# An mLSTM head's output transposes moved from behind the third to behind the fourth output-gate unit

## The reference

```python
hm = mlstm_chunkwise(mq, mk, mv, i_pre, logf)
hm = hm * lax.rsqrt(jnp.mean(hm * hm, axis=-1, keepdims=True) + EPS)
hm = (hm.reshape(B, S, M_WIDTH) * m_norm_w[l]).astype(x.dtype)
hm = hm * jax.nn.sigmoid(mo)
y_m = (hm * jax.nn.silu(mz)) @ w_m_branch[l]
```

## Time and profile before

| what | value |
|---|---|
| time, median of 3 runs | 1391.82 us (1391.68 to 1391.87) |
| time of the profiled execution | 1391.64 us |
| its span, first to last instruction | 1389.9 us |
| mean granted TensorE clock | 0.992 |
| tensor engine busy | 1328.2 us, 96% |
| vector engine busy | 668.1 us, 48% |
| ScalarE busy | 397.0 us, 29% |
| GpSimd busy | 662.6 us, 48% |

### The profile page before, as it was taken

The page is one execution under the profiler, slowest core; times in us unless marked ns, Lnnn a source line. Parts: engine busy times, 40 slices in busy tenths (PEclk is TensorE's granted clock), DMA queues, the critical chain, the costliest instruction groups (busy, mean ns, idle before and its releaser), DMA issues.

```text
span 1389.9 us, 20009 instructions
## 1 busy us (share of the span) xinstructions
PE 1328.2 (96%) x6846; PEld 1128.8 (81%) x6846; DVE 668.1 (48%) x1297; ACT 397.0 (29%) x926; POOL 662.6 (48%) x854
## 2 busy tenths in 40 slices
PE   3499999999999999999999999999999999999997
PEld 2398797989877888889978987898789888688886
DVE  5979886785873000153265235424542321544335
ACT  5334445353450100023322332333132311311111
POOL 6834507061366544295267146715661455557340
PEclk9799999999999999999999999999999999999999
DMA  9411102010021220230131031103210132321502
GB/s 350 123 45 31 47 2 61 15 32 28 0 61 61 75 79 26 89 93 17 48 89 30 0 90 46 30 0 92 59 30 15 45 92 91 106 91 61 197 16 106
DMA packets 119832, 89.30 MB, mean 64 GB/s; under 512 B 13305, under 2 KB 111721, under 8 KB 118894
## 3 DMA queue, kind: packets, MB, share of 16 engines
q1 hardware_dynamic: 116288, 76.16, 17.9%
q10 hardware_dynamic: 3502, 12.61, 2.6%
HBM read 80.35 MB, written 8.41 MB: 64 GB/s over the span
## 4 chain that ended last, share of the span: by engine, by line
PE 82%; DVE 12%; issue 2%; ACT 2%; DVEq 0%; ACTq 0%
PE pp L532 24%; PE pp L533 23%; PE pp L534 23%; PE pp L718 2%; PE pp L728 2%; PE pp L638 1%; DVE y_lo L1294 1%; DVE prob L1237 1%; DVE num L1404 1%; PE pp L710 1%; PE pp L621 1%; PE pp L629 1%; PE pp L723 1%; PE pp L622 1%; PE pp L607 1%
## 5 line engine op out<-in xcount | busy, mean ns | idle before, releaser
L484 POOL TENSOR_TENSOR w_hi<-raw,ones 128x256 fp32r<-128x256 f32 x404 | 284.1, 734 | 619.1 <-ACTq L346 341.0
L532 PE MATMUL pp<-h_hi,w_hi 128*128 128x512 f32 x912 | 361.5, 396 | 9.9 <-DVE h_lo L1120 8.3
L533 PE MATMUL pp<-h_lo,w_hi 128*128 128x512 f32 x912 | 356.1, 390 | 0.0
L534 PE MATMUL pp<-h_hi,w_lo 128*128 128x512 f32 x912 | 355.9, 390 | 0.0
L488 POOL TENSOR_TENSOR w_lo<-raw,w_hi 128x256 fp32r<-128x256 f32 x404 | 345.7, 887 | 7.9
L532 PEld LDWEIGHTS pp<-h_hi,w_hi 128*128 128x128 f32 x912 | 171.8, 188 | 49.6 <-issue 6.8
L534 PEld LDWEIGHTS pp<-h_hi,w_lo 128*128 128x128 f32 x912 | 171.8, 188 | 36.0
L533 PEld LDWEIGHTS pp<-h_lo,w_hi 128*128 128x128 f32 x912 | 171.9, 188 | 34.6
L532 PE MATMUL pp<-w_hi,h_hi 128*128 128x384 f32 (+1 forms) x512 | 162.1, 317 | 0.6 <-DVE roped L1214 0.6
L534 PE MATMUL pp<-w_hi,h_lo 128*128 128x384 f32 (+1 forms) x512 | 158.1, 309 | 0.0
L533 PE MATMUL pp<-w_lo,h_hi 128*128 128x384 f32 (+1 forms) x512 | 158.0, 309 | 0.0
(11 more groups left out here) (216 smaller groups left out, 1855.9 us busy)
## 6 DMA issues: line engine op xcount, KB each, us to landing
raw<-w_in SPq DMA_DIRECT2D x72, 512.0 KB, 3.6
w_mod<-w_ada SPq DMA_DIRECT2D x7, 1024.0 KB, 11.5
x_in<-x SPq DMA_DIRECT2D x4, 1024.0 KB, 8.0
raw<-w_att SPq DMA_DIRECT2D x8, 512.0 KB, 5.0
merged_dram<-mix_a ACTq DMA_DIRECT2D x8, 512.0 KB, 2.6
w_gate<-w_ada ACTq DMA_DIRECT2D x8, 512.0 KB, 3.4
raw<-w_m SPq DMA_DIRECT2D x8, 512.0 KB, 3.6
mix_in<-merged_dram ACTq DMA_DIRECT2D x8, 512.0 KB, 3.3
```

The source lines that it names most:

```text
L484: ins = pool.tensor_tensor(hi[:, q, :], raw[:, s, q, :], one[:, q, :], ALU.mult)
L532: pe.matmul(o, lh, rh, start=first, stop=False)
L533: pe.matmul(o, lh, rl, start=False, stop=False)
L534: return pe.matmul(o, ll, rh, start=False, stop=last)
```

## The change

In the tensor engine's program the condition under which the 16 transposes are issued changes from the third to the fourth of the output gate's units:

```diff
@@ -747,7 +747,7 @@
                         chunk(i, n - 1)
                     if (kind, n) == ("mo", 0):
                         chunk(i, NB - 1)
-                    if (kind, n) == ("mo", 2):
+                    if (kind, n) == ("mo", 3):
 
                         after(pe, k_weighted, NB * (i + 1))
                         for q in range(4):
```

## The result

The changed kernel takes 1400.82 us (median of 6 runs, 1400.18 to 1401.61), against 1391.84 for the kernel before (6 runs, 1391.68 to 1392.15): 9.0 us or 0.64% slower, ratio 1.0064 with a 95% interval of 1.0052 to 1.0076. The prediction said 1397.1, with a range of 1395.9 to 1401.7, so direction and range hold for this measurement. The likeliest case, +5.3 us with the clock kept, is not what came: its 5.3 us are there, and the first rival's clock falls lie on top of them.

A forecast was written before the change was run, and what follows sets the result against it. The tensor engine, busy for 96% of the span, was taken to bound the kernel. Transposes losing their cover add 3 x 1.76 = 5.3 us, head 3 adds 0: 1391.82 + 5.3 = 1397.1 us, range 1395.9 to 1401.7.

The forecast's parts named there:

- The likeliest case: Whole kernel: 5.3 us slower, 1397.1 us, with the clock kept at 1.00; chance 0.62.
- the first rival: Heads 0 to 2: clock falls in the empty hole before mo3, 2.3 us a head, 1399.4 to 1404.0; chance 0.27.
- The wait for the normalised outputs vanishes: Transposes, now behind mo3, no longer wait: outputs are ready from 705.99, transposes come after 713.
- The wait for mo3's bank does not move: Head 0: mo3 starts at 707.80 again, behind mo1's sigmoid; the tensor engine's hole before it is 3.00 us, now empty.
- The transposes cost 1.76 each head: Behind mo3 the 16 transposes lose their cover: 1.76 us a head (1.52 to 2.14), 5.3 in heads 0 to 2.
- step 5: After head 0's transposes: vector engine's products and ScalarE's xpad come later anyway, covered by 0.4 and 5 us.
- Head 3 costs nothing: Head 3: mo3's bank is free in time, so mo3 and the transposes swap places at the same sum: 0.
- the sum: Whole kernel: 1.76 us in each of heads 0 to 2, +5.3 us on the median 1391.82, giving 1397.1.
- The two other rivals: Vector engine earlier, mo3's bank wait gone too, 1387.6 us, chance 0.03; later slack returns the 5.3, 1391.8 us, chance 0.05.

The follow-up runs named there:

- both fillings: The changed kernel with 16, or with 4, identity transposes that nobody reads ahead of mo3's bank wait: 1399.31 us and 1398.49 us.
- the first repetition: The changed kernel measured again without any edit: 1401.86 us, 6 runs from 1398.39 to 1404.32, ratio 1.0072.

## Why the prediction was right, and where it was short

1. *The wait for the normalised outputs vanishes.* Right: no entry of L757 is left.
2. *The wait for mo3's bank does not move.* Right: mo3's first matmul starts 3.38 to 3.39 us behind mo2's last in head 0 before, in all three profiles of the changed kernel, and in both fillings, and the waits are 3.0 us in heads 0 to 2. To mo3's second start it is 3.72 us, but 3.97 where the clock was low already at the restart (head 1 of the changed kernel: 845.86, lasting 0.80). The chain that I named, eight normalisations, gate product, sigmoid, bank, was shown from both sides: taking the product out of it removed the wait (1387.23), and shortening what lies ahead of it by 1.8 us shortened the wait by as much (1392.11).
3. *The transposes cost 1.76 each head.* Right: 2.21 less 0.45 again, behind mo3. No reader of them is late: in head 0 they end at 717.18, and the vector engine reads them at 717.53, behind its last gate product, as step 5 had it.
4. *Head 3 costs nothing.* Right: no wait in it, before or after.
5. *The clock.* Here the forecast was short. The forecast with the clock kept was given 0.62, and a fall in one to three heads 0.27. In the three profiles of the changed kernel two, two and one of three holes were followed by the low clock, and none of its 17 executions took 1397.1 us; the fastest took 1398.31. The argument that failed is the one against the rival, that no fall came in an idle time of 2.2 us (1202 to 1204). That row was one execution's luck: behind the same idle time, where the tensor engine then works in short bursts, the clock fell 0.4 to 1.8 us after the restart in nine of the 14 profiles, the changed kernel's among them (0.91 over 1205 to 1225), and stayed in five. The rule of the Trainium skill that I set against the sum (TensorE: Matmul & The Clock Gate, "Why this matters for your kernels": no idle gaps over about 3 us) was the better guide here. A hole of 3.0 us is enough to lose the clock, in some executions and not in others.
6. *The price and the range.* A fall cost 1.4 to 1.6 us, not 2.3: I had taken that from a restart after a much longer idle time, with ten slow steps, where seven to nine came. Taken together, 5.3 + 2 x 1.5 is 8.3 against 9.0 measured. The upper end of the range, 1401.7, was two falls at the price that was too high, and this 1.6 us too much covered the 0.7 us that the sum lacks. So that the first median, 1400.82, lies inside is in part luck; that of the first repetition, 1401.86, lies 0.2 us outside.

The two other rivals did not come by themselves. The vector engine was not earlier (706.17 to 707.38 for the product, 0.26 later like all of this execution), and nothing gave the 5.3 us back. Falls of the clock outside the four heads, at 146 us above all, were in no term.

## What to carry to other kernels

Before moving work off a wait, ask which wait ends last at that place, and whether the work was filling it: a wait for A that vanishes in front of a wait for B gains nothing, and what lay between becomes an added cost. Look for the root that both waits share, here one vector instruction that stood behind eight others it did not need. Moving that alone gained 2.4 us, moving the tensor engine's work alone lost 9.0, and both together gained 4.8. And an empty hole near 3 us can cost more than itself, through the clock of what follows.

## What the runs showed of the hardware that was not expected

- Less work was slower: without its 64 transposes the kernel before took 2.7 us more. With transposes of the identity in the hole, 16 or 4, the granted clock stayed at 1.00 behind six of six; and 16 transposes alone, at 45.33 to 48.98 us, were followed by a rise from 0.50 to 1.00 in the kernel before.
- The fall of the clock is not settled by the idle time's length alone: of nine holes of 3.0 us in three profiles of the changed kernel five were followed by 1.2 GHz and four were not, and behind 2.2 us it fell in nine of 14 profiles. It fell also at 146 us, in eight of 14, where no idle time shortly before it was longer than 1.5 us. What decides between equal places stays open; no run was made for it.
- A low-clock period cost the same program 1.4 to 1.6 us when it met full matmuls, 2.8 in one case of the kernel without transposes, 0.2 to 1.7 at 146 us (as found in the start of head 0's last gate units), and nothing when the tensor engine was following the vector engine anyway.
- The 128x1 step of the vector engine (L1355) takes 0.16 us as the median of its 32 times in the kernel before, 0.54 beside GpSimd's split of 128x256 in head 3, and 2.33 beside its one addition of 128x1024, which lasts 2.41: it ends when that addition ends. Moving the addition took the 1.8 us away.
